# Gate and up weights of an expert in one transfer, down weights in a ring of their own, in both expert layers

## The reference, cut to what matters

```python
# h: tokens x 1024; 64 experts of width 256, the best 8 for each token
def expert_block(args):
    tok, e = args
    xb = h_pad[tok]
    a = jax.nn.silu(xb @ w_gate[e]) * (xb @ w_up[e])
    return a @ w_down[e]
...
routed = jnp.zeros((n_tok + 1, d), h.dtype).at[slot_tok].add(y)[:n_tok]
shared = (jax.nn.silu(h @ s_gate) * (h @ s_up)) @ s_down
return routed + shared
```

## Time and profile before

| what | us |
|---|---|
| median of 3 executions | 3268.34 |
| lowest, highest | 3265.45, 3277.77 |
| the profiled execution, its own time | 3282.85 |
| its span in the trace | 3281.0 |
| mean granted clock of TensorE | 0.978 |
| PE busy in the span | 3051.5 (93%) |
| DVE busy | 1951.5 (59%) |
| transfers of experts issued, layer 0 | 1822.0 to 2434.5 |
| transfers of experts issued, layer 1 | 2729.6 to 3227.1 |

### The profile page before, as it was taken

The page is one execution under the profiler, slowest core; times in us unless marked ns, Lnnn a source line. Parts: engine busy times, 40 slices in busy tenths (PEclk is TensorE's granted clock), DMA queues, the critical chain, the costliest instruction groups (busy, mean ns, idle before and its releaser), DMA issues.

```text
span 3281.0 us, 54765 instructions
## 1 busy us (share of the span) xinstructions
PE 3051.5 (93%) x22527; PEld 2253.7 (69%) x22527; DVE 1951.5 (59%) x2734; ACT 674.7 (21%) x1267; POOL 246.1 (7%) x259
## 2 busy tenths in 40 slices
PE   8998799999999889999988999999998989998887
PEld 8997589999999668899956543333337767543443
DVE  7977777787987877788676641111116655533332
ACT  1013323200001433211123311111112142111111
POOL 0100200010100110011100011111100000000000
PEclk9999899999999899999999999999999999999998
DMA  6554434454444542354310479999987314999995
GB/s 249 188 185 178 171 110 144 159 195 184 180 180 159 212 155 108 137 193 180 129 39 26 179 273 421 420 418 416 416 359 290 116 65 175 403 420 421 421 421 227
DMA packets 93339, 764.77 MB, mean 233 GB/s; under 512 B 12816, under 2 KB 13840, under 8 KB 24208
## 3 DMA queue, kind: packets, MB, share of 16 engines
q1 hardware_dynamic: 79392, 719.42, 55.9%
q0 software_dynamic: 13680, 41.70, 3.3%
HBM read 746.38 MB, written 25.17 MB: 235 GB/s over the span
## 4 chain that ended last, share of the span: by engine, by line
PE 63%; DMA 16%; DVE 14%; ACT 3%; SPq 2%; issue 2%; DVEq 0%; POOL 0%; ACTq 0%; POOLq 0%
PE ps L489 62%; DMA ring<-wexp_dram 14%; DVE ring_r L436 2%; PE ps L508 2%; SPq L3144 1%; DVE ring_r L435 1%; DVE ring_r L454 1%; DMA arena<-wexp_dram 1%; DMA ring<-yd_dram 1%; SPq L3141 1%; DVE ring L1427 1%; DVE arena L2376 1%; DVE arena L1300 0%; DVE arena L1278 0%; ACT ring_r L448 0%
## 5 line engine op out<-in xcount | busy, mean ns | idle before, releaser
L489 PE MATMUL ps<-arena_r,ring_r 128*128 128x256 f32 (+1 forms) x9776 | 1282.5, 289 | 36.0 <-DVE ring_r L436 15.5
L489 PEld LDWEIGHTS ps<-arena_r,ring_r 128*128 128x128 f32 x9776 | 1224.1, 190 | 70.1 <-DVE ring_r L436 15.7
L489 PE MATMUL ps<-ring,arena 128*32 128x512 f32 (+3 forms) x4080 | 688.9, 572 | 61.5 <-DMA ring<-wexp_dram 56.3
L489 PEld LDWEIGHTS ps<-ring,arena 128*32 128x32 f32 (+3 forms) x4080 | 206.5, 120 | 429.4 <-issue 302.3
L489 PE MATMUL ps<-arena 128*32 128x512 f32 (+8 forms) x2464 | 410.1, 429 | 55.4 <-DVE ring L1427 16.2
L436 DVE TENSOR_TENSOR ring_r<-ring,ring_r 128x4096 fp32r<-128x4096 f32 (+2 forms) x104 | 445.4, 4283 | 3.6
L489 PEld LDWEIGHTS ps<-arena 128*32 128x32 f32 (+3 forms) x2464 | 216.0, 167 | 180.1 <-issue 79.3
L435 DVE CAST ring_r<-ring 128x4096 fp32r<-128x4096 f32 (+2 forms) x104 | 256.2, 2463 | 57.7 <-PE ps L489 45.8
L3046 DVE TENSOR_TENSOR arena<-arena,ps 128x256 f32<-128x256 f32 x42 | 17.7, 421 | 330.1 <-ACT arena L3077 330.1
L508 PEld LDWEIGHTS ps<-consts_sb,arena 128*128 128x128 f32 (+1 forms) x787 | 89.5, 142 | 85.5 <-issue 64.6
L489 PE MATMUL ps<-consts_sb,arena 128*32 128x512 f32 (+5 forms) x432 | 135.4, 531 | 4.0 <-DMA consts_sb<-wexp_dram 4.0
(11 more groups left out here) (403 smaller groups left out, 2788.6 us busy)
## 6 DMA issues: line engine op xcount, KB each, us to landing
ring<-wexp_dram SPq DMA_DIRECT2D x293, 1024.0 KB, 20.1
ring<-stream_dram SPq DMA_DIRECT2D x138, 2048.0 KB, 7.8
arena<-wexp_dram SPq DMA_DIRECT2D x62, 1024.0 KB, 29.8
consts_sb<-wexp_dram SPq DMA_DIRECT2D x29, 1024.0 KB, 20.4
ring<-yd_dram SPq DMA_DIRECT2D x4, 2048.0 KB, 12.3
arena<-yd_dram SPq DMA_DIRECT2D x2, 2048.0 KB, 11.2
ring<-stream_dram SPq DMA_DIRECT2D x3, 1024.0 KB, 5.1
consts_sb<-consts_dram SPq DMA_DIRECT2D x1, 2245.0 KB, 15.9
```

The costliest lines, as they stand in the source:

```text
L489: return pe.e.matmul(ps, lhsT=lhsT, rhs=rhs, start=start, stop=stop, skip_group_check=True)
```

## The change

In both layers parts a and b of an expert become one item "ab": one transfer of 2 MB, 16 KB a row, into a double slot. Part d goes to a second ring of slots of 1 MB. Both rings have their own turns, but the items stay in one order in SP's one queue: ab of the set's new experts, then the d of the same set (layer 1) or of the set before (layer 0). Layer 0 has five pairs and six singles (16 MB), layer 1 four pairs and three singles (11 MB); the slot that was used once is gone. A pair is free when part b was used (the end of the hidden product), and PE waits for the whole pair ahead of step 0. Three of the pairs are free from the start, the fourth (and in layer 0 the fifth) when the last shared up product is done.

```diff
+                self.paired = l in PAIRED
+                self.once = 0 if b0 or self.paired else 1
...
+                parts = ("ab",) if self.paired else "ab"
                 for i in range(self.n + 1):
                     if i < self.n:
-                        self.items += [(part, p) for part in "ab" for p in new[i]]
+                        self.items += [(part, p) for part in parts for p in new[i]]
...
+                self.turn_of, counts = {}, [0, 0]
+                for part, p in self.items:
+                    ring = int(self.paired and part == "d")
+                    self.turn_of[part, p] = ring, counts[ring]
+                    counts[ring] += 1
...
+                early = [(CT_, cplan["dc"][0])]
+                rows, normed = [[(arena, r.base + 2048 * j) for j in (0, 1)] for r in (HT, Ur)]
+                if self.paired:
+                    pairs = list(zip([ring_of[0], hi_of[0], hi_of[2], ring_of[2]], last * 3 + gate_up))
+                    singles = list(zip(ring_of[5:] + early, before + last))
+                    if l == 0:
+                        pairs += list(zip(normed[0:1], gate_up))
+                        singles += list(zip(rows + [(arena, OH[0].base)], [("rows", l)] * 2 + [("weighted", l)]))
+                    return pairs, singles + list(zip(ring_of[4:5], down))
...
+            def before(self, part, p):
+
+                ring, i = self.turn_of[part, p]
+                j = i - len(self.homes()[ring]) + (0 if ring else self.once)
+                if i < len(self.homes()[ring]):
+                    return None
+                return next(it for it in self.items if self.turn_of[it] == (ring, j))
+
+            def item(self, part, p):
+                return ("ab" if self.paired and part != "d" else part), p
...
             def raw(self, part, p):
-                of, o = self.homes()[self.home(self.place[part, p])][0]
+                ring, i, _ = self.home(*self.item(part, p))
+                of, o = self.homes()[ring][i][0]
+                o += 2048 * (self.paired and part == "b")
                 return of[:, o:o + 2048]
...
-            homes = S.homes()
-            for i, (part, p) in enumerate(S.items):
-                if i >= S.once + S.slots:
-                    eng.wait_ge(*at(S.key, "used", *S.items[i - S.slots]))
+            for part, p in S.items:
+                ring, i, _ = S.home(part, p)
+                before = S.before(part, p)
+                if before is not None:
+                    eng.wait_ge(*at(S.key, "used", before[0][-1], before[1]))
                 elif not b0:
-                    eng.wait_ge(*at(*homes[i][1]))
+                    eng.wait_ge(*at(*S.homes()[ring][i][1]))
...
-                o = 2048 * "abd".index(part)
-                sp.dma_start(S.raw(part, p), src[:, o:o + 2048]).then_inc(S.weights[S.home(i)], 16)
+                o, n = 2048 * "abd".index(part[0]), 2048 * len(part)
+                of, at_ = S.homes()[ring][i][0]
+                sp.dma_start(of[:, at_:at_ + n], src[:, o:o + n]).then_inc(S.arrival(part, p), 16)
```

More of the change, by code:

```diff
@@ L2876, in dve_route @@
             dve.here("dve", "experts", l)
+        PAIRED = (0,1)
         class Sets:
@@ L2887, in __init__ @@
                 self.done, self.weights, self.x, self.y = SEC[l, b0]
-                self.once = 0 if b0 else 1
-                self.slots = len(self.weights) - self.once
+                self.paired = l in PAIRED
+                self.once = 0 if b0 or self.paired else 1
                 new, old = [], set()
@@ L2914, in homes @@
                 once = [(arena, (XG[1] if l else sub(14336, 2048)).base)] if self.b0 == 0 else []
                 homes = list(zip(once, last))
-                homes += list(zip(ring_of[5:] + ring_of[0:2] + hi_of + [(CT_, cplan["dc"][0])], before + last * 7))
+                homes += list(zip(ring_of[5:] + ring_of[0:2] + hi_of + early, before + last * 7))
                 if l == 0:
-                    homes += list(zip([(arena, HT.base + 2048 * j) for j in (0, 1)], [("rows", l)] * 2))
+                    homes += list(zip(rows, [("rows", l)] * 2))
@@ L2919, in homes @@
                 homes += list(zip(ring_of[2:4], gate_up * 2))
                 if l == 0:
[L2921 to L2926, removed]
+                    homes += list(zip(normed + [(arena, OH[0].base)], gate_up * 2 + [("weighted", l)]))
@@ new lines, in homes, with home @@
+                return homes + list(zip(ring_of[4:5], down)), []
+            def home(self, part, p):
+                ring, i = self.turn_of[part, p]
+                once = 0 if ring else self.once
+                size = len(self.homes()[ring]) - once
+                return ring, i if i < once + size else once + (i - once) % size, 1 if i < once else (i - once) // size + 1
+            def before(self, part, p):
+                ring, i = self.turn_of[part, p]
+                j = i - len(self.homes()[ring]) + (0 if ring else self.once)
+                if i < len(self.homes()[ring]):
+                    return None
+                return next(it for it in self.items if self.turn_of[it] == (ring, j))
@@ L2928, in raw, with arrival @@
+            def item(self, part, p):
+                return ("ab" if self.paired and part != "d" else part), p
             def raw(self, part, p):
-                of, o = self.homes()[self.home(self.place[part, p])][0]
+                ring, i, _ = self.home(*self.item(part, p))
+                of, o = self.homes()[ring][i][0]
+                o += 2048 * (self.paired and part == "b")
                 return of[:, o:o + 2048]
+            def arrival(self, part, p):
+                ring, i, _ = self.home(part, p)
+                return self.weights[i + ring * len(self.homes()[0])]
@@ L2932, in got @@
             def got(self, part, p):
-                i = self.place[part, p]
-                return self.weights[self.home(i)], 16 * (1 if i < self.once else (i - self.once) // self.slots + 1)
+                it = self.item(part, p)
+                return self.arrival(*it), 16 * self.home(*it)[2]
             def got_x(self, i):
@@ L2948, in all_done @@
                     eng.wait_ge(*at(self.key, who, "end"))
-                for it in self.items[-self.slots:]:
+                last_of = {self.arrival(*it): it for it in self.items}
+                for it in last_of.values():
                     eng.wait_ge(*self.got(*it))
```

## The result

The changed kernel takes **3323.94 us** (median of 4, 3317.15 to 3331.02) against 3270.36 (4 runs of the kernel before): a ratio of 1.0146, 95% interval 1.0123 to 1.0169, or 48 us slower (40 to 55); the two medians by themselves are 53.6 us apart. The forecast was +41 and 3309, the range up to 3328: the time lies inside, 4 us from its upper end. The profiled execution took 3322.91 us, its span 3321.1.

A forecast was written before the change was run, and what follows sets the result against it. Both expert layers were taken as bound by DMA, PE not far behind. Layer 1's start, ten rounds of 40.5 us and tail gave +41.7, layer 0 -1: +41 on the median, 3309 us, range 3264 to 3328.

The forecast's parts named there:

- Start of layer 1: Layer 1's first sets: pairs 4, 5, 6 stand behind d3, putting set 4's hidden product at 2856.5 us.
- The round: Layer 1, two sets: 14.9 us to the down product's end plus 23.2 to the third pair, 38.1 against 38.0.
- two downs 4.98: Layer 1's round, after the down product's end: the next set's two down transfers take 4.98 us of the 23.2.
- The clock: Layer 1, three-expert sets: a PE gap of about 4.9 us brings the 1.2 GHz clock, costing 2.4 us a round.
- Sum: Layer 1: set 4 at 2856.5, ten rounds of 40.5 us, then 17.6 and 14.9, ending at 3294.0: +41.7 us.
- the tail: End of layer 1: 17.6 us to set 25's last pair and 14.9 more, with 3.5 us extra in it.
- rival 2: Layer 1: the loop binds but the clock costs nothing; 3285 us, or 3280 with the early ends; chance 0.20.
- Layer 0: Larger packets -6.4 us, missing slot +2.5, later pair release 0 to 3.5: -3.9 to -0.4, taken as -1.
- The level: Whole kernel: the profiled difference of +41 us carried over to the median of 3268.34, giving 3309 us.
- Rival 3: Both layers: pairs move at the old rate, 16 KB rows cut in two again; +51 us, 3319; chance 0.07.
- Rival 4: Layer 0: its ring of five pairs starves too, 1 us for each of 42 sets; 3350 us; chance 0.05.
- Rival 1: Both layers: the DMA never runs dry and each keeps 6.4 us; -7 us, 3261, not slower; chance 0.15.

The follow-up runs named there:

- busy_gap: The changed kernel plus matmuls nobody reads, 5 before each three-expert set's hidden product in layer 1 and 10 after its second pair lands; ratio to before 1.0098.
- l0_only: The changed kernel with pairs in layer 0 only, layer 1 as in the kernel before; ratio to before 0.9995.
- reorder: The changed kernel with SP issuing layer 1's next-set pairs whose slots an earlier set has used ahead of this set's downs; ratio to before 0.9999.
- start_order: The changed kernel with the order of reorder for the first two sets of layer 1 only; ratio to before 1.0131.
- reorder_8k: The kernel reorder with each pair in two 1 MB transfers (8 KB rows) on one semaphore; ratio to before 1.0030.

## Why the prediction was right

**Start of layer 1: right.** d3 waits for set 0's down product and the pairs stand behind it. The sum put set 4's hidden product at 2856.5, 126.9 us after the first transfer at 2729.6; it was 127.2 (2719.15 to 2846.35). That the two agree so well is in part luck: set 2's first down release came sooner than forecast (its next transfer was issued 103.5 us after the first, at 2822.60, for 104.4), and the way from there to set 4 was 1.3 us longer (23.7 for 22.5).

**The round: right in kind, 1.2 us too short.** The prediction had 14.9 from hidden start to the end of the down product, and 23.2 from there to the third pair. In the round shown the first is 17.95 (3052.92 to 3070.87), of which 2.9 is the clock (9.93 against 7.05, the same x58 at 2.4 GHz in the row below), so 15.1; the second is 24.35 (3070.87 to 3095.22). In this round the term that is too small is thus "two downs 4.98", on a queue that has just been empty. The landings of the first and the second down, by their own line's view:

```profile
DMA to landing us min/median/max: 4.9/4.9/4.9
...
DMA to landing us min/median/max: 7.7/7.7/7.7
```

The first was issued at 3071.7 and landed at 3076.6, the time of the earlier trace rows; the second, issued at 3072.8, landed at 3080.5, 3.9 us later and not 2.5. The pairs then landed 4.9 apart (3085.4, 3090.3, 3095.2), so this 1.4 us stays to the end. But the round shown is the one with the largest such step. Over the ten rounds the second down landed 2.5 to 3.9 us after the first, 3.0 on average, and in four rounds it was the second pair that came late, 5.9 to 6.1 us after the first pair in place of 4.9. What holds for all: from the first down's landing to the third pair's it took 17.2 to 19.0 us, 18.2 on average, where the sum has 17.4. So of the 1.2 us a round that are missing, 0.8 lie in the transfers behind the restart, about 0.3 in PE's part and 0.1 in the first down. Why the place of the delay changes from round to round is not shown.

With the clock taken out, the mean round is 41.4 − 2.1 = 39.3 and that of `busy_gap` 39.5, against 38.1.

**The clock: right in kind, a little too dear.** The prediction had one gap of 4.9 us. In eight of the ten rounds it is two, of 1.8 to 2.9 and of 3.0 to 3.9 us, with a pair of matmuls of 1.0 to 1.9 us between them; in the other two there is a gap of 4.4 or of 3.9 us and none over 0.6 before it. Every one of the ten has a stretch at a lower clock. Windows behind three of them, the lowest, the highest and the one at the end of the round shown, and then the same x58 without a long gap ahead of it:

```profile
3011.80:3017.80 6.00, 6.00 (x32) 1.41 (x36) 0.00 (x0) 0.00 (x0) 0.00 (x0) 0.50 1.05 440
2970.40:2976.40 6.00, 6.00 (x44) 1.55 (x48) 0.00 (x0) 0.00 (x0) 0.00 (x0) 0.75 1.05 438
3095.30:3101.30 6.00, 6.00 (x36) 1.47 (x40) 0.00 (x0) 0.00 (x0) 0.00 (x0) 0.63 1.04 436
```

```profile
2865.94 7.05 PE L489 MATMUL ps<-ring,arena 128*32 128x512 f32 x58 [1.61 <-DMA ring<-wexp_dram]
```

A granted clock of 0.50 is the 1.2 GHz level throughout, 0.63 and 0.75 are that level for three quarters and for half of the 6 us. The x58 of the ten sets after set 4 took 8.57 to 10.03 us, 9.15 on average: 2.1 over 7.05, where the prediction took 2.4 between 0 and 2.9. `busy_gap` gave 1.9 a round. The Trainium skill ("TensorE: Matmul & The Clock Gate", HAM oscillation) has a DMA wait before each tile leave every tile cold; this trace agrees for the three-expert sets, in all ten rounds. It does not for the two-expert set of the row above, which waited 1.61 us and ran at full clock.

**Sum.** Start +0.3, ten rounds +8.6 (413.6 for 405), the tail 32.5 as forecast (3259.97 to 3292.4, for 17.6 + 14.9): 573.3 for 564.4. Had the clock cost nothing, rival 2 would have been right in kind and about 12 us too low.

**Layer 0: within its bounds, sign open.** Forecast −1, between −3.9 and −0.4. Five profiled executions with the same paired layer 0 (after, l0_only, reorder, busy_gap, start_order) give 908.7 to 912.8, two with the old one 907.6 and 908.4; by time `l0_only` is −0.05% (−6 to +2 us). That the slots take what the larger packets gain there, as the sum had it, was not taken apart: the difference can't be told from 0.

**The level.** 3309 came from moving the +41 onto a median of 3268; the kernel took 3324, 15 us more. Of these the median of before is 2, which moved up with a fourth run; the traces place 9 in layer 1 (573.3 for 564.4) and 2 in layer 0 (+1.1 for −1), and the rest is inside what single executions differ by.

**Rival 3 has the right number and is wrong.** It gave +51 for pairs that move at the old rate, and the trace has 50.6 in layer 1. But in a full queue the pairs landed 4.9 us apart, 2 MB at 428 GB/s and not at 421, and `reorder_8k` shows that rows or count are worth 10 us. **Rival 4** (layer 0 starves too, 1 us for each of 42 sets) is ruled out by the 1.1 us of that layer.

**Rival 1 is what the change could have been.** Its place, a DMA that never runs dry, is `reorder`; its price was too good. I had −7 and `reorder` measures 0 (−5 to +4), layer 1 being 1.2 us longer than before at 423 GB/s in place of 421. The 10 us of the rows (or of the count) are real by `reorder_8k`. Part of what takes them back can be read from the rows. In `reorder` the gather behind set 4's hidden product starts 127.6 us after the layer's first transfer (2723.37), in the kernel before it was 121.4 (2851.03, 2729.63):

```profile
2851.01 2.17 PE L489 MATMUL ps<-arena_r 128*128 128x256 f32 x16
```

So the start costs 6.2 us. And at the tail the last down product ends 14.2 us after the last wait for gate and up weights, where it was 10.8, so 3.4 us, the term for which the prediction had 3.5. What lies between that gather and that last wait wins 8.5 us back. The rows of `reorder`, then that of before (its last down is in the earlier trace rows):

```profile
3233.02 7.08 PE L489 MATMUL ps<-ring,arena 128*64 128x512 f32 x30 [0.23 <-DMA ring<-wexp_dram]
3243.58 3.65 PE L489 MATMUL ps<-ring,arena 128*64 128x512 f32 x16
```

```profile
3241.52 3.65 PE L489 MATMUL ps<-ring,arena 128*64 128x512 f32 x14 [1.40 <-DMA ring<-wexp_dram]
```

## What to carry to other kernels

Before two uses of one ring are split, write down SP's order and ask of each wait what stands behind it: a load that could go must not queue behind one whose slot is released later. Coarser transfers cost nothing in the rounds while the queue was never empty, and some us at the start and the end of the layer. Compare the loop "release, issue, latency, transfers, compute" with the DMA's own time per round; where they are level, the restart of an empty queue and the clock after the gap are paid in every round, as they were here.

## What the runs showed of the hardware

- A queue that had run empty needed more than its latency: the first 1 MB landed 4.9 us after its issue, and the next 1 MB and three times 2 MB took 18.2 us more on average of ten rounds (17.2 to 19.0), where the rates of a full queue give 17.1 to 17.4. The second 1 MB came 2.5 to 3.9 us behind the first, for 2.5 in a full queue.
- Gaps in PE's work of up to 1.6 us, often two in a row, left the granted clock of the window at 0.99 (`reorder`, three short stretches at 1.2 GHz). Gaps of 1.8 to 2.9 and 3.0 to 3.9 us with 1.0 to 1.9 us of matmuls between them brought 0.50 to 0.75 over the next 6 us, each time (`after`). A short burst in the middle of a wait did not hold the clock; matmuls all through the wait, 7 us of them, did (`busy_gap`, 1.00).
- Equal layers 0 differed by up to 4 us from one profiled execution to the next, and equal code ahead of them by up to 14, so a single trace settles a few us only where the same row repeats.
